# Bank order of the panels, and small work moved in its queues, in a two-layer decoder trunk

## The chip, the cores and the metric

One core of one Trainium2 chip. The metric is the device time of one execution in microseconds (us). Three runs of the kernel before gave 1307.50, 1307.45 and 1304.81: median 1307.45.

## What is computed

A decoder trunk of two layers on 512 tokens of width 1024, in float32. Layer one is gated linear attention, layer two stick-breaking attention on keys and values of its own projection; each is followed by a mixture of 16 experts (top group, two experts of it). Cut to what matters here:

```
def gla_mixer(u, w_in, w_gk2, b_gk2, o_norm, w_out):      # u = rms_norm(h, a_norm)
    q, k, v, gk_lr, g = split(u @ w_in, [512, 1024, 2048, 2064])
    gk = log_sigmoid(gk_lr @ w_gk2 + b_gk2) / 16           # gk_lr has 16 columns
    b = cumsum(gk) in chunks of 64
    q_dec, k_inv, k_to_end = q * exp(b) * 128**-0.5, k * exp(-b), k * exp(b_last - b)
    att = tril(q_dec @ k_inv.T)
    o = att @ v + q_dec @ state;  state = exp(b_last) * state + k_to_end.T @ v
    return (rms_norm(o, o_norm) * silu(g)) @ w_out
h = h + gla_mixer(...);  h = h + hier_moe(rms_norm(h, m_norm[0]), ...)
k1, v1 = split(rms_norm(h, kv_norm) @ w_kv)
h = h + stick_breaking(rms_norm(h, b_norm) @ b_w_q, k1, v1) @ b_w_out
h = h + hier_moe(rms_norm(h, m_norm[1]), ...);  out = rms_norm(h, final_norm)
```

## The kernel before

The program is written out by hand, one instruction stream for each engine, with semaphores between them. Every product of a large matrix is made of three: an operand is rounded to the type float32r (`hi`, by ACT) and its residual is kept as a second operand (`lo`, by DVE), and PE adds hi*hi, lo*hi and hi*lo (`three`, L1272). Weights come in blocks of 1 MB (4 tiles of 128 rows by 512 columns), loaded by SP into four slots `raw` (L411), rounded by ACT's `split` (L463) and completed by DVE's `split` (L811); the factor of the norm gain is multiplied in there, four instructions of 512 columns each. A weight without a gain takes one instruction of 2048 columns.

A panel is a product with 512 output columns: two blocks, 96 matmuls, and four PSUM banks. `dense(p, c, feature_major)` (L1340) computes panel p from blocks c and c+1 and writes banks 0 to 3 for even p and 4 to 7 for odd p. ACT's `panel_out_tokens` (L538) or DVE's `panel_out_features` (L879) copies it out, times the reciprocal norm: of a token for the first, by a row that is broadcast over the partitions (`rstd_row`) for the second. In layer one the panels are 0 (values, first half), 1 (queries), 2 (keys), 3 (values, second half), 4 and 5 (output gate), and 6 and 7 (output projection). The 16-column low-rank input of the forget gates is computed inside panel 0's function, and the gates (`wgk2`, L1382) after it, into banks 4 to 7, from where DVE adds the bias (L918).

The first panel of a layer is `dense_first` (L1317): token tiles of x (or h) are transposed by PE one at a time (`transposed_tile`, L1300), rounded by ACT (`tile_hi`, L529) and completed by DVE (`tile_lo`, L874), and each is followed by its two half products (blocks c and c+1, 12 matmuls each). Before the last tile's halves stands `between()`: in layer one the low-rank products and then the factor sums `rstd_row_sums` (L1309), in layer two the sums alone. The sums need the squares of all tokens (ACT, L522), the reciprocal root (ACT and DVE) and four diagonal tiles (DVE, L854); they write bank 6, and ACT copies the row out (L536). The products of panel 0 don't need them.

At the start ACT's queue issues nine small loads (L480): five rows of norm gains, then the low-rank weight `lr_raw`, `wgk2`, the gate bias `bgk` and `onorm`. PE first transposes the gains (L1362), then token tile 0. After layer one's panels come 16 transposes of the keys (L1398, banks 0 to 3) and 16 score products (L1405, banks 4 to 7); ACT copies the transposed keys (L595), DVE the scores (L950), which it writes over the untransposed keys. In layer two panels 12 and 13 are the two halves of the queries; DVE copies the second (L1202) behind the residual of block 13, and the early scores (`early_scores`, L1617) need only the first half, the late ones (`late_scores`, L1630) both.

Each engine takes its instructions in the order written; a wait holds all that stands behind it in the same queue.

## Time and profile before

| | |
|---|---|
| median of three runs | 1307.45 us |
| the profiled execution | 1304.74 us, span 1303.1 us |
| PE busy | 1136.8 us, 87% of the span |
| DVE, ACT, POOL busy | 819.4, 694.4, 157.1 us |
| granted PE clock, mean | 0.936 |
| moved by DMA | 283.49 MB, mean 218 GB/s |

The profile is of one execution. Its times count from the start of the span; 1.6 us lie around the span. An engine's idle time is put down to the instruction that released it. L12 is line 12 of the kernel before. In a row of the timeline the first number is the start and the second the time to the end of the group, x8 the number of records in it (a float32 matmul leaves more than one), and the bracket the idle time of the engine ahead of it with what ended it. The granted clock is the share of full speed that PE's throttle let through: 1.00 is 2.4 GHz, 0.50 is 1.2 GHz.

### The profile page before, as it was taken

What the parts mean: (1) busy time and instruction counts of PE and PEld (TensorE: products, weight loads), DVE (VectorE), ACT (ScalarE), POOL (GpSimd) and SP (SyncE); (2) the same over time, 40 slices, a digit from 0 to 9 for tenths busy, and PEclk for the clock granted to TensorE, in tenths of its full rate; (3) what the DMA queues carried; (4) which work ended last, traced back from release to release, by engine and by line L of the source; (5) the groups of instructions that cost most, each with busy time, mean ns of one, the idle gap of its engine ahead of it and who ended that gap; (6) DMA issues with size and microseconds to landing.
All of it is one profiled execution on the core that took longest, in us unless ns stands there. A gap on an engine that the chain in (4) does not pass through costs nothing.

```text
span 1303.1 us, 14486 instructions
## 1 busy us (share of the span) xinstructions
PE 1136.8 (87%) x5477; PEld 859.9 (66%) x5477; DVE 819.4 (63%) x825; ACT 694.4 (53%) x732; POOL 157.1 (12%) x169
## 2 busy tenths in 40 slices
PE   5799997974999999995799989999839999999970
PEld 4488875853677777774578867767626777777740
DVE  2454236266888888885523346662568888888846
ACT  2442433243777777775233226662427777777742
POOL 1100030012010100001100004430030010010004
PEclk9899998985999999998799988999859999999995
DMA  8343103207999999996412210003069999999925
GB/s 282 79 145 130 33 1 117 77 17 235 385 391 393 403 392 392 403 371 243 147 65 98 97 33 1 1 17 129 1 222 374 394 399 390 393 394 411 380 75 193
DMA packets 89060, 283.49 MB, mean 218 GB/s; under 512 B 11704, under 2 KB 11872, under 8 KB 89008
## 3 DMA queue, kind: packets, MB, share of 16 engines
q1 hardware_dynamic: 70272, 239.09, 48.5%
q0 software_dynamic: 11024, 39.07, 9.0%
q10 hardware_dynamic: 7712, 4.63, 1.1%
q8 instruction: 34, 0.56, 0.2%
q14 instruction: 18, 0.15, 0.0%
HBM read 259.96 MB, written 22.81 MB: 217 GB/s over the span
## 4 chain that ended last, share of the span: by engine, by line
PE 77%; DVE 7%; issue 5%; POOL 4%; ACT 3%; DMA 2%; ACTq 1%; POOLq 0%; DVEq 0%
PE ps L1274 23%; PE ps L1276 23%; PE ps L1275 23%; PE ps L1458 2%; PE ps L1292 1%; POOL xn_r L1829 1%; DMA xn<-output_table,pos 1%; PE ps L1419 1%; DVE h L1170 1%; PE ps L1486 1%; DVE raw L1214 1%; DVE xn_r L1218 1%; DMA pad<-normed_rows,token 1%; POOL xn_r L1824 1%; POOL pad_r L1824 1%
## 5 line engine op out<-in xcount | busy, mean ns | idle before, releaser
L816 DVE TENSOR_TENSOR w_lo<-raw,w_hi 128x2048 fp32r<-128x2048 f32 x72 | 164.7, 2289 | 94.8 <-ACT w_hi L470 94.6
L470 ACT CAST w_hi<-raw 128x2048 fp32r<-128x2048 f32 x72 | 137.7, 1912 | 117.7 <-PE ps L1276 117.5
L1274 PE MATMUL ps<-xT_hi,s_hi 128*96 128x512 f32 (+1 forms) x392 | 157.0, 400 | 8.6 <-DVE s_lo L910 5.2
L816 DVE TENSOR_TENSOR xT_lo<-raw,xT_hi 128x2048 fp32r<-128x2048 f32 x64 | 146.1, 2288 | 20.4 <-ACT xT_hi L470 20.4
L1274 PE MATMUL ps<-w_hi,s_hi 128*96 128x512 f32 x384 | 154.7, 403 | 4.6 <-DVE s_lo L992 4.6
L1276 PE MATMUL ps<-xT_hi,s_lo 128*96 128x512 f32 (+1 forms) x392 | 155.5, 397 | 0.0
L1275 PE MATMUL ps<-xT_lo,s_hi 128*96 128x512 f32 (+1 forms) x392 | 154.7, 395 | 0.0
L1276 PE MATMUL ps<-w_hi,s_lo 128*96 128x512 f32 x384 | 152.9, 398 | 0.0
L1275 PE MATMUL ps<-w_lo,s_hi 128*96 128x512 f32 x384 | 152.1, 396 | 0.0
L470 ACT CAST xT_hi<-raw 128x2048 fp32r<-128x2048 f32 x64 | 122.0, 1912 | 38.3 <-PE ps L1276 38.3
L1274 PE MATMUL ps<-w_hi,xT_hi 128*128 128x512 f32 x304 | 122.1, 401 | 12.9 <-DVE w_lo L820 6.4
L820 DVE SCALAR_TENSOR_TENSOR w_lo<-raw,gainT,w_hi 128x512 fp32r<-128x512 f32 x88 | 60.0, 746 | 114.8 <-ACT w_hi L474 114.8
L1275 PE MATMUL ps<-w_lo,xT_hi 128*128 128x512 f32 x304 | 120.3, 396 | 0.0
L1276 PE MATMUL ps<-w_hi,xT_lo 128*128 128x512 f32 x304 | 120.1, 395 | 0.0
L474 ACT ACTIVATE w_hi<-raw,gainT 128x512 fp32r<-128x512 f32 x88 | 56.1, 713 | 117.5 <-PE ps L1276 117.5
L816 DVE TENSOR_TENSOR w_lo<-xn,w_hi 128x2048 fp32r<-128x2048 f32 x32 | 73.4, 2292 | 28.9 <-ACT w_hi L470 28.9
L1274 PEld LDWEIGHTS ps<-xT_hi,s_hi 128*96 128x96 f32 (+1 forms) x392 | 63.4, 162 | 35.3 <-issue 6.7
L1274 PEld LDWEIGHTS ps<-w_hi,s_hi 128*96 128x96 f32 x384 | 63.4, 165 | 30.4 <-DVE s_lo L992 5.6
L816 DVE TENSOR_TENSOR xT_lo<-xn,xT_hi 128x2048 fp32r<-128x2048 f32 x32 | 73.4, 2292 | 15.7 <-ACT xT_hi L470 15.7
L1276 PEld LDWEIGHTS ps<-xT_hi,s_lo 128*96 128x96 f32 (+1 forms) x392 | 62.8, 160 | 28.6 <-issue 1.1
L1276 PEld LDWEIGHTS ps<-w_hi,s_lo 128*96 128x96 f32 x384 | 62.6, 163 | 27.5
L1275 PEld LDWEIGHTS ps<-xT_lo,s_hi 128*96 128x96 f32 (+1 forms) x392 | 63.1, 161 | 26.5 <-issue 0.9
(282 smaller groups left out, 2004.9 us busy)
## 6 DMA issues: line engine op xcount, KB each, us to landing
raw<-in_m_w_up SPq DMA_DIRECT2D x64, 1024.0 KB, 10.5
xn<-in_m_w_gate SPq DMA_DIRECT2D x60, 1024.0 KB, 11.6
raw<-in_m_w_down SPq DMA_DIRECT2D x60, 1024.0 KB, 11.2
raw<-in_a_w_in SPq DMA_DIRECT2D x12, 1024.0 KB, 5.9
output_table<-pad POOLq DMA_DIRECT2D x32, 384.0 KB, 6.4
raw<-in_w_kv SPq DMA_DIRECT2D x8, 1024.0 KB, 7.4
raw<-in_a_w_out SPq DMA_DIRECT2D x4, 1024.0 KB, 5.7
raw<-in_m_w_gate SPq DMA_DIRECT2D x4, 1024.0 KB, 8.8
```

The lines of the kernel that those rows point to most:

```text
L470: se.copy(hi, raw_block).then_inc(A["hi_done"], 1)
L474: ins = se.activation(hi[:, cols], raw_block[:, cols], ACT.Copy, scale=gainT[:, n:n + 1])
L816: ve.tensor_tensor(lo, raw_block, hi, ALU.subtract).then_inc(V["lo_done"], 1)
L820: ins = ve.scalar_tensor_tensor(lo[:, cols], raw_block[:, cols], gainT[:, n:n + 1], hi[:, cols], ALU.mult, ALU.subtract)
L1170: ve.scalar_tensor_tensor(h[:, i, :], y_rows[n], w12[:, k, i:i + 1], h[:, i, :], ALU.mult, ALU.add).then_inc(V["combined"], 1)
L1214: ve.scalar_tensor_tensor(zt[part], z_of(q, part), 0.0, zt[part], ALU.max, ALU.add).then_inc(V["L_done"], 1)
L1218: ve.tensor_tensor(L_of(L_lo, q, part), zt[part], L_of(L_hi, q, part), ALU.subtract).then_inc(V["L_lo_done"], 1)
L1274: te.matmul(o, a_hi, b_hi, start=start, stop=False)
L1275: te.matmul(o, a_hi, b_lo, start=False, stop=False)
L1276: return te.matmul(o, a_lo, b_hi, start=False, stop=stop)
L1458: ins = te.transpose(ps[:, 4 + f, CAP * k:CAP * (k + 1)], xg[:, slot, pair_columns(4 * f + k)], ident[0:CAP, 0:CAP])
L1824: ge.tensor_copy(L_of(L_hi, q, part), zt[part]).then_inc(G["L_hi_done"], 1)
```

## The change

Loads and transposes at the start: the four loads of the low-rank weight, `wgk2`, bias and `onorm` are issued by SP behind the x tiles and ahead of block 2, not by ACT. PE transposes token tile 0 before the gains, and ACT and DVE handle that tile before they need the gains. The rounding and residual of the low-rank weight come directly after block 1 on ACT and DVE, ahead of token tile 1. ACT's squares of a tile follow the rounding of the next one. In `dense_first` the low-rank products stay ahead of the last tile's halves and the factor sums go between the two halves, in both layers.

Bank order: layer one's panels are numbered 0, 2, 3, 4, 5, 6, so that queries go to banks 0 to 3, directly after the gates in banks 4 to 7, and all later ones alternate; each wait goes with its panel. The scores are computed before the keys are transposed, and DVE waits for the transposes before it writes scores over the keys. In layer two the second query copy stands ahead of the residual of block 13.

```diff
@@ sync
             for i in range(NT):
...

+            for dst, src in ((lr_raw, a_w_in[0, :, GK0:GK0 + RANK]...), (wgk2, a_w_gk2[0]),
+                             (bgk, a_b_gk2[0]...), (onorm, a_o_norm[0].partition_broadcast(P))):
+                sp.dma_start(dst, src).then_inc(A["small_loaded"], 16)
@@ scalar
-            load_small(loads, A["small_loaded"])
...
+            tile_hi(0, 0)
             act.wait_ge(V["gains_out"], 1)
-            tile_hi(0, 0)
             split(0)
             split(1)
+            act.wait_ge(V["lr_scaled"], 1)
+            se.copy(lr_hi, lr_raw[:, :, :]).then_inc(A["lr_hi_done"], 1)
             for i in range(1, NT):
                 tile_hi(0, i)
-            norm_squares(0)
-            act.wait_ge(V["lr_scaled"], 1)
-            se.copy(lr_hi, lr_raw[:, :, :]).then_inc(A["lr_hi_done"], 1)
+                squares_of(0, i - 1)
+            squares_of(0, NT - 1)
+            rsqrt_first(0, NT)
             split(2)
...
-            panel_out_tokens(3, 7, v[:, :, BN:2 * BN])
+            panel_out_tokens(4, 7, v[:, :, BN:2 * BN])
-            panel_out_tokens(4, 9, sg[:, :, 0:BN], ACT.Silu)
+            panel_out_tokens(5, 9, sg[:, :, 0:BN], ACT.Silu)
-            panel_out_tokens(5, 11, sg[:, :, BN:2 * BN], ACT.Silu)
+            panel_out_tokens(6, 11, sg[:, :, BN:2 * BN], ACT.Silu)
@@ vector
+            tile_lo(0, 0)
             dve.wait_ge(M["gains_tr"], 1)
             ve.tensor_copy(gainT[:, :], ps[:, 7, 0:5 * KT]).then_inc(V["gains_out"], 1)
             dve.wait_ge(V["gains_out"], 1)
-            tile_lo(0, 0)
             split(0)
             split(1)
-            for i in range(1, NT):
-                tile_lo(0, i)
             dve.wait_ge(A["small_loaded"], 16 * SMALL)
             ve.tensor_tensor(lr_raw...).then_inc(V["lr_scaled"], 1)
+            dve.wait_ge(A["lr_hi_done"], 1)
+            ve.tensor_tensor(lr_lo, lr_raw[:, :, :], lr_hi, ALU.subtract).then_inc(V["lr_lo_done"], 1)
+            for i in range(1, NT):
+                tile_lo(0, i)
             norm_scale(0)
             diagonals()
-            dve.wait_ge(A["lr_hi_done"], 1)
-            ve.tensor_tensor(lr_lo, lr_raw[:, :, :], lr_hi, ALU.subtract).then_inc(V["lr_lo_done"], 1)
             split(2)
...
-            panel_out_features(1, 3, qT, DK ** -0.5)
+            panel_out_features(2, 3, qT, DK ** -0.5)
-            panel_out_features(2, 5, kT)
+            panel_out_features(3, 5, kT)
...
             for n in range(8, 14):
                 split(n)
+            dve.wait_ge(M["ktok_tr"], 1)
             for i in range(NT):
                 dve.wait_ge(M["att_done"], i + 1)
...
             split(B + 12)
+            panel_out_features(13, B + 11, qT1[:, 4:8, :], SD ** -0.5)
             split(B + 13)
-            panel_out_features(13, B + 11, qT1[:, 4:8, :], SD ** -0.5)
@@ tensor
-            def dense_first(p, c, turn, event, between):
+            def dense_first(p, c, turn, event, first, between, between_half):
                 transposed_tile(turn, event, 0)
+                first()
                 for j in range(NT):
                     if j == NT - 1:
                         pe.wait_ge(V["xT_lo_done"], XT[turn] + NT)
                         between()
                     half(j, 0)
                     if j < NT - 1:
                         transposed_tile(turn, event, j + 1)
+                    else:
+                        between_half()
                     half(j, 1)
...
-            dense_first(0, 0, 0, 0, low_rank)
+            dense_first(0, 0, 0, 0, gains_transposed, low_rank, token_factors)
             pe.wait_ge(V["lr_out"], 1)
...
+            pe.wait_ge(A["panel_out"], 1)
+            dense(2, 2, True)
             pe.wait_ge(V["gates_in"], GH)
-            dense(1, 2, True)
-            pe.wait_ge(A["panel_out"], 1)
-            dense(2, 4, True)
+            dense(3, 4, True)
             pe.wait_ge(V["qk_out"], 1)
-            dense(3, 6, False)
+            dense(4, 6, False)
             pe.wait_ge(V["qk_out"], 2)
-            dense(4, 8, False)
+            dense(5, 8, False)
             pe.wait_ge(A["panel_out"], 2)
-            dense(5, 10, False)
-            pe.wait_ge(V["k_toend"], 1)
+            dense(6, 10, False)
+            pe.wait_ge(V["k_inv"], 1)
             pe.wait_ge(A["panel_out"], 3)
...
-                    ins = te.transpose(ps[:, i, P * j:P * (j + 1)], kT[:, j, P * i:P * (i + 1)], ident[:, :])
-            ins.then_inc(M["ktok_tr"], 1)
-            pe.wait_ge(V["k_inv"], 1)
-            pe.wait_ge(A["panel_out"], 4)
...
-            pe.wait_ge(V["k_inv"], 1)
-            pe.wait_ge(A["panel_out"], 4)
                     ins = te.matmul(ps[:, 4 + i, P * j:P * (j + 1)], kinv[:, j, t], qT[:, j, t], start=True, stop=True)
                 ins.then_inc(M["att_done"], 1)
+            pe.wait_ge(V["k_toend"], 1)
+            pe.wait_ge(A["panel_out"], 4)
...
+                    ins = te.transpose(ps[:, i, P * j:P * (j + 1)], kT[:, j, P * i:P * (i + 1)], ident[:, :])
+            ins.then_inc(M["ktok_tr"], 1)
...
-            dense_first(8, B, 3, 2, lambda: rstd_row_sums(2))
+            dense_first(8, B, 3, 2, lambda: None, lambda: None, lambda: rstd_row_sums(2))
```

## Rows read from the trace of the kernel before

**Rows 1.** The page, part 4: share of the chain that ended last, by engine.
```profile
PE 77%; DVE 7%; issue 5%; POOL 4%; ACT 3%; DMA 2%; ACTq 1%; POOLq 0%; DVEq 0%
```

**Rows 2.** Waits of PE over the whole span: total us, times, longest us.
```profile
PE ps L1362 <- DMA pad<-in_m_norm: 7.9, 1, 7.9
...
PE ps L1274 <- DVE s_lo L910: 5.2, 1, 5.2
PE ps L1608 <- DVE pad L883: 5.2, 1, 5.2
...
PE ps L1274 <- DVE pad L918: 2.8, 1, 2.8
...
PE ps L1313 <- DVE pad L854: 1.9, 1, 1.9
```

**Rows 3.** The chain in order of time, 0 to 90 us: start us, us, what.
```profile
3.16 0.43 ACTq L480
...
4.97 3.97 ACTq L480
8.97 1.20 ACT L557
10.27 1.01 ACT xT_hi L531
11.28 2.46 ACT w_hi L474 x4
13.76 2.75 DVE w_lo L820 x4
...
35.80 4.17 ACT xn L522 x8
41.46 0.88 DVE pad L854 x4
...
43.70 0.43 PE ps L1276
```

**Rows 4.** Time by engine, 87 to 174.5 us: busy us (count), clock, DMA share, GB/s.
```profile
87.00:174.50 87.50, 87.50 (x388) 72.42 (x387) 35.14 (x36) 27.78 (x40) 0.00 (x0) 1.00 0.19 61
```

**Rows 5.** Timeline of PE, 42 to 64 us: start, us, operation, idle before.
```profile
42.68 0.59 PE L1274 MATMUL ps<-xT_hi,s_hi 128*16 128x512 f32 x1 [5.17 <-DVE s_lo L910]
...
50.31 1.05 PE L1313 MATMUL ps<-pad,neg_one 128*128 128x128 f32 x8
...
56.75 3.70 PE L1382 MATMUL ps<-pad 16*128 16x512 f32 x8
63.27 0.80 PE L1274 MATMUL ps<-xT_hi,pad_r 128*128 128x512 f32 x1 [2.82 <-DVE pad L918]
```

**Rows 6.** Timeline of DVE, first and second layer's panels.
```profile
87.45 2.29 DVE L883 SCALAR_TENSOR_TENSOR pad<-ps,pad 128x2048 f32<-128x2048 f32 x1 [8.46 <-PE ps L1276]
...
770.68 2.29 DVE L816 TENSOR_TENSOR w_lo<-raw,w_hi 128x2048 fp32r<-128x2048 f32 x1 [8.57 <-ACT w_hi L470]
772.89 2.28 DVE L883 SCALAR_TENSOR_TENSOR pad<-ps,pad 128x2048 f32<-128x2048 f32 x1
```

**Rows 7.** Line L418, the four token tiles of x (issued 0.95 to 3.66).
```profile
DMA to landing us min/median/max: 3.7/11.0/12.2
```

**Rows 8.** Timeline of PE, 173 to 182 us.
```profile
174.29 1.91 PE L1398 MATMUL ps<-ident,pad 128*128 128x128 f32 x16
177.06 3.81 PE L1405 MATMUL ps<-pad 128*128 128x128 f32 x32 [0.86 <-ACT raw L542]
```

**Rows 9.** Line L414, weight blocks 0 and 1 (issued 1.39 and 1.86).
```profile
DMA to landing us min/median/max: 6.0/7.7/9.4
```

**Rows 10.** DMA issues, 0 to 80 us: name, queue, count, KB, us to landing.
```profile
pad<-in_a_o_norm ACTq DMA_DIRECT2D x1, 128.0 KB, 16.2
...
lr_raw<-in_a_w_in ACTq DMA_DIRECT2D x1, 64.0 KB, 13.3
```

**Rows 11.** Timeline of ACT: the copy of the first panel.
```profile
56.86 2.42 ACT L542 ACTIVATE pad<-ps,rstd 128x512 f32<-128x512 f32 x4
```

More of the change, by code:

```diff
@@ L421, in _ @@
                     load(streams[0][1], 1)
+            with nc.allow_non_contiguous_dma(reason="512 gate biases and 16 columns a row"):
+                for dst, src in ((lr_raw[:, :, :], a_w_in[0, :, GK0:GK0 + RANK].rearrange("(k p) r -> p k r", p=P)),
+                                 (wgk2, a_w_gk2[0]), (bgk[:, :], a_b_gk2[0].rearrange("(h p) -> p h", p=P)),
+                                 (onorm, a_o_norm[0].partition_broadcast(P))):
+                    sp.dma_start(dst, src).then_inc(A["small_loaded"], 16)
             for layer in range(LAYERS):
@@ L484, in _ @@
             load_small(loads, A["gains_loaded"])
-            loads = [(lr_raw[:, :, :], a_w_in[0, :, GK0:GK0 + RANK].rearrange("(k p) r -> p k r", p=P))]
-            loads += [(wgk2, a_w_gk2[0]),
-                      (bgk[:, :], a_b_gk2[0].rearrange("(h p) -> p h", p=P)),
-                      (onorm, a_o_norm[0].partition_broadcast(P))]
             router_loads = []
@@ L1357, in dense, with gains_transposed @@
                     ins.then_inc(M["blk_used"], 1)
+            def gains_transposed():
+                pe.wait_ge(A["gains_loaded"], 16 * 5)
+                te.transpose(ps[:, 7, 0:5 * KT], gain_rows, ident[0:5 * KT, 0:5 * KT]).then_inc(M["gains_tr"], 1)
             pe.wait_ge(G["consts"], 1)
-            pe.wait_ge(A["gains_loaded"], 16 * 5)
-            te.transpose(ps[:, 7, 0:5 * KT], gain_rows, ident[0:5 * KT, 0:5 * KT]).then_inc(M["gains_tr"], 1)
             def gate_input(k):
@@ L1375, in low_rank, with token_factors @@
                     gate_input(k)
+            def token_factors():
                 pe.wait_ge(G["consts"], 2)
                 rstd_row_sums(0)
-            dense_first(0, 0, 0, 0, low_rank)
+            dense_first(0, 0, 0, 0, gains_transposed, low_rank, token_factors)
             pe.wait_ge(V["lr_out"], 1)
@@ L1383, in _ @@
             ins.then_inc(M["gates_done"], 1)
+            pe.wait_ge(A["panel_out"], 1)
+            dense(2, 2, True)
             pe.wait_ge(V["gates_in"], GH)
-            dense(1, 2, True)
-            pe.wait_ge(A["panel_out"], 1)
-            dense(2, 4, True)
+            dense(3, 4, True)
             pe.wait_ge(V["qk_out"], 1)
-            dense(3, 6, False)
+            dense(4, 6, False)
             pe.wait_ge(V["qk_out"], 2)
-            dense(4, 8, False)
+            dense(5, 8, False)
             pe.wait_ge(A["panel_out"], 2)
-            dense(5, 10, False)
-            pe.wait_ge(V["k_toend"], 1)
+            dense(6, 10, False)
+            pe.wait_ge(V["k_inv"], 1)
             pe.wait_ge(A["panel_out"], 3)
-            for i in range(NT):
-                for j in range(GH):
-                    ins = te.transpose(ps[:, i, P * j:P * (j + 1)], kT[:, j, P * i:P * (i + 1)], ident[:, :])
-            ins.then_inc(M["ktok_tr"], 1)
-            pe.wait_ge(V["k_inv"], 1)
-            pe.wait_ge(A["panel_out"], 4)
             for i in range(NT):
@@ L1406, in _ @@
                 ins.then_inc(M["att_done"], 1)
+            pe.wait_ge(V["k_toend"], 1)
+            pe.wait_ge(A["panel_out"], 4)
+            for i in range(NT):
+                for j in range(GH):
+                    ins = te.transpose(ps[:, i, P * j:P * (j + 1)], kT[:, j, P * i:P * (i + 1)], ident[:, :])
+            ins.then_inc(M["ktok_tr"], 1)
             ktok = gate
```

## The prediction

> **What bounds the kernel now.** The first view is the page's chain of work that ended last: 77% of it is PE, and no other engine has more than 7% [rows 1]. So time is won where PE stands still, or where it runs at the lower of its two clock levels; work taken off ACT or DVE counts only if PE waits for it. The second view, PE's waits, shows where it stands still near the edited lines [rows 2]: 7.9 us at the very start until the norm gains have landed; 5.2 us before the low-rank product, which waits for the small weight's residual (L910); 2.8 us before panel 1, which waits for the gates to be read out of banks 4 to 7 (L918); in the second layer 1.9 us before the factor sums (L1313), and 5.2 us before the late scores (L1608), which wait for the second query copy. Each is a single wait, so each can be priced by itself.
>
> The third view is the chain in order of time for the first 90 us [rows 3]. It shows what stands ahead of the first matmul: ACT's queue issues the small loads from 3.16 us and is held by the last until 8.94, then loads its function table (1.2), rounds token tile 0 (1.0), rounds block 0 (2.5), and DVE forms the residual (2.75): PE's first product starts at 16.5. Later it shows four squares of 4.2 us together, and factor tiles that end at 42.3, just ahead of the low-rank product.
>
> **The clock.** From 87 to 174.5 us PE is busy without a gap at a granted clock of 1.00, and four panels of 96 products take 87.5 us [rows 4], 0.228 each: that is the 2.4 GHz level. Behind the 5.2 us of idle time a product took 0.43 [rows 3], the 1.2 GHz level, and the 24 low-rank products lasted from 42.68 to 50.31, 7.6 us [rows 5]. At 0.228 they take 5.5, so the drop cost 2.2. Behind the 2.8 us of idle time panel 1 lasted from 63.27 to its copy at 87.45 [rows 5, 6], 24.2 us where 96 times 0.228 is 21.9: 2.3 lost.
>
> **The change, part by part.**
>
> *Start.* Four loads leave ACT's queue, and PE transposes token tile 0 before the gains. The table load can begin near 3.2 and ends by 4.5. Token tile 0 lands at 0.95 + 3.7 = 4.65 [rows 7]. Eight transposes at the lower level: 16 took 1.91 at the full one [rows 8], so 8 take 1.9 here, to 6.6. ACT rounds the tile until 7.6; DVE's residual of the tile, half of a 2.29 us operation [rows 6] and a little, ends near 8.9. The gains still land at 7.9 [rows 2] on the same queue, are transposed by 8.2 and copied by DVE after the tile, to 9.1. Block 0 landed at 7.4 and block 1 at 11.3 [rows 9], and block 1 is wanted at 11.6. So 9.1 + 2.5 + 2.75 [rows 3] puts the first product at 14.5 in place of 16.5: 2.0 won. The bounds: 0 if the gains land over 2 us later, 3 if DVE's two steps are hidden. I take 2.0, by the durations.
>
> *Small loads in SP's queue.* They now stand behind x tiles 1 to 3 and ahead of blocks 2 and 3. The last x tile lands at 3.66 + 12.2 = 15.9 [rows 7]. Blocks 2 and 3 are wanted only after 36 us, so their delay costs nothing. The small loads cost nothing if they are in before ACT is wanted for token tile 1: in the new order DVE has finished block 1 at 14.5 + 2.75 = 17.2, scaling and splitting the low-rank weight takes about 0.9 on both engines, and PE's first half block (12 products, 2.7 to 5.1 us at the two levels) and the transposes end between 18 and 20.5. The limit for landing is therefore about 19. I take the loads of one queue to land in the order of their issue, as the x tiles do (3.7 us for the first, 12.2 at the most). With 0.2 MB behind the 15.9 I expect 17 to 18.5, cost 0; it was 13.3 to 16.2 us from issue to landing for two of them on ACT's queue, beside the large loads [rows 10], and that is the upper bound: 29 to 32 us. Behind a late landing, token tile 1's rounding on ACT and its residual on DVE would both queue, and PE behind them. The Trainium skill (DMA: Bandwidth & Descriptors, Queues, rings and completion order) speaks against this move: each queue has its own ring on an engine, rings are served in turn and each one in its own order, so a small load in a queue of its own shares from the first packet, and one behind 4 MB waits for them. By it the loads land behind the last x tile and not before, where in their own queue they could have come sooner; the sum by it is the same as long as they make the limit. The trace agrees on the turns only in part: the separate queue still needed 13 to 16 us.
>
> *Low-rank split and squares moved ahead.* The weight's residual is ready before 20 us, and token tile 3's residual before PE gets there, so the 5.2 us wait goes, and with it the 2.2 of lower clock. Next late would be the factor sums. On the old time axis PE is through with its third tile at 37.5, low-rank ends at 43.0, the first half of tile 3 (12 products) at 45.7. Of the 4.2 us of squares, half now lies beside PE's work, so the factor tiles end near 40.2 rather than 42.3 [rows 3]: covered by 5 us. The sums (0.9) end at 46.6; ACT's copy of the row factor and DVE's scaling of the low-rank result (together about 1.3, an estimate from their 512 columns) end at 47.9, and PE needs them at 49.3.
>
> *Panel 2 before 3.* The gate products take 3.7 [rows 5], to 53.0. The query panel goes into banks 0 to 3, which ACT must have emptied: row factor copied at 47.2, block 3 rounded (2.5) by 49.7, panel copy (2.42 [rows 11]) by 52.2. That is 0.8 ahead of PE. The wait of 2.8 goes, and 2.3 of lower clock. If the cover fails, PE waits by the excess alone. DVE, though, starts the gate chain only 7.5 us earlier (53.0 for 60.5) while the panel's end comes 12.5 earlier; it had 8.46 idle before its copy [rows 6], so 3.4 are left and nothing is late. The later panels keep the alternation they had, and their copies shift with them.
>
> *Scores before key transposes.* The transposes took 1.91 and the scores 3.81 [rows 8]. Scores now start at once, and transposes end 174.4 + 3.8 + 1.9 = 180.1. ACT comes to the transposed keys after a panel copy (2.4), a block (1.9) and a table (1.2), at about 180.0. DVE's new wait for the transposes stands before its attention copies, behind a block that it finishes later than 180.1. I charge 0.2; bounds 0 and 0.5. The 0.86 and the following 1 us of PE's idle time become one gap of 2.
>
> *Second layer.* The factor sums move behind a half tile (2.7 us), which covers the 1.9 wait [rows 2]: 1.9 won. The second query copy (2.28) goes ahead of a block residual that waited for ACT: before, 770.68 + 2.29, then the copy to 775.17 [rows 6]; ACT's rounding began 1.9 before 770.68, at 768.8, so now 768.8 + 2.28 + 2.29 = 773.4. The attention chain starts 1.8 earlier. PE's late scores start 4.2 earlier, but DVE leads that chain: I take 1.8, bounds 0 and 3 (a better clock in the first pair).
>
> **The sum.** 2.0 + 5.2 + 2.2 + 2.8 + 2.3 - 0.2 + 1.9 + 1.8 = 18.0. The profiled execution took 1304.7 (span 1303.1 and 1.6 around it), which gives 1286.7; the median of the three runs is 1307.45, 2.7 higher, which gives 1289.4. I state 1288. A measurement of this kernel can tell about 0.2%, 2.6 us.
>
> **The rivals.**
> 1. *Small loads late* (13%, of which 3% slower than before). Place: DVE's wait before the low-rank scaling. Price: 1 us for each us past 19. At the bound of 29 to 32 it is 10 to 13: 1298 to 1301. It ends slower only from a landing past 37, and by over 0.2% past 40: 1310. For it: 13 to 16 us on the old queue. Against it: only 0.2 MB, and no large load beside it in another queue.
> 2. *The clock falls in the attention of layer one* (12%), at the merged gap of 2 us. For it: the drop behind 2.8. Against it: in the second layer 1.9 of waiting cost no visible drop. Price one or two drops of 2.2: 1290 to 1292.5.
> 3. *The clock terms do not come*, because a cover of 0.8 or 3.4 us fails and new short waits stand there (10%): 4.5 less, 1292.5.
> 4. *It does not do what it says*: the gain is given back, since a later stage is tied to loads (3%): 1305 to 1308. Against it: the loads wait for slots that DVE frees, and the chain has 2% DMA [rows 1].
> 5. *More than forecast* (5%): 1282 to 1284, by the upper bounds of start and query copy.
>
> The forecast itself has 57%: 1285 to 1291. With rivals 2, 3 and 5 and the nearer half of rival 1 the range is 1282 to 1296. Faster 0.94, same 0.02, slower 0.04 (3% of rival 1, 1% unforeseen).
>
> **What would show it.** First product near 14.5; no wait at L910 or L918; low-rank products all near 0.23; first query copy on DVE near 73 in place of 87.45; DVE's first absolute value after the second query copy 1.8 earlier relative to the panel's end. Wrong: a wait of PE or ACT behind the low-rank scaling, a product of 0.43 behind a panel boundary, or a first layer that is less than 12 us shorter.

## The result, and the profile after

| | before | changed |
|---|---|---|
| median of 4 runs each | 1306.27 us | 1290.05 us (1289.15 to 1291.36) |
| the profiled execution | 1304.74 | 1291.36 |
| its span, granted clock | 1303.1, 0.936 | 1289.7, 0.939 |

The ratio is 0.9877, interval 0.986 to 0.9894: the change makes the kernel faster by 16.2 us by the medians. The profiled execution of the changed kernel is the slowest of its four and that of the kernel before lies below its median, so the two traces differ by 13.4 us only; the landmarks below are accounted against that. A landmark is the start of one step that both kernels have. The page of the changed kernel, part 1 (busy time of each engine) and part 4 (the chain):

```profile
PE 1134.4 (88%) x5477; PEld 859.7 (67%) x5477; DVE 819.5 (64%) x825; ACT 694.4 (54%) x732; POOL 156.2 (12%) x169
...
PE 79%; DVE 7%; issue 5%; POOL 4%; DMA 3%; ACT 3%; POOLq 0%; DVEq 0%; ACTq 0%
```

PE's share of the chain is 79% where it was 77 [rows 1], ACT's queue is at 0%. PE's waits of the changed kernel, the answers to [rows 2]:

```profile
PE ps L1661 <- POOL xn_r L1839: 6.8, 1, 6.8
PE ps L1277 <- DVE w_lo L822: 6.6, 1, 6.6
...
PE ps L1309 <- DMA h<-in_x: 4.4, 1, 4.4
...
PE ps L1429 <- ACT pad L597: 2.2, 1, 2.2
...
PE ps L1618 <- DVE pad L885: 1.0, 1, 1.0
```

None is left on the low-rank residual, on the gates or on the factor tiles. The late scores of the second layer wait 1.0 in place of 5.2. In exchange the first factor product of the second layer's first pair waits 6.8 for POOL (1.9 before), and the state products of layer one wait 2.2 in one piece for ACT's copy of the transposed keys.

The timeline of PE, changed kernel, the start (start us, us, line, shape, count, idle before), answering to [rows 5]:

```profile
14.27 0.80 PE L1277 MATMUL ps<-w_hi,xT_hi 128*128 128x512 f32 x1 [6.55 <-DVE w_lo L822]
...
19.55 1.41 PE L1309 MATMUL ps<-ident,h 128*128 128x128 f32 x8
...
36.26 0.40 PE L1277 MATMUL ps<-xT_hi,s_hi 128*16 128x512 f32 x1
...
44.57 1.05 PE L1316 MATMUL ps<-pad,neg_one 128*128 128x128 f32 x8
...
48.28 4.52 PE L1392 MATMUL ps<-pad 16*128 16x512 f32 x8
52.74 0.79 PE L1277 MATMUL ps<-xT_hi,pad_r 128*128 128x512 f32 x1
...
57.95 0.40 PE L1277 MATMUL ps<-xT_hi,pad_r 128*128 128x512 f32 x1
```

The first product starts at 14.27 (16.56 before). The first half block and the transposes last until 20.71. The low-rank products follow at 36.26 without a wait and take 5.57 to 41.83, at 0.23 each. The gate products start at 48.28 (56.75), the query panel at 52.74 (63.27), directly behind them. But its first products again take 0.43, and only from 57.95 do they take 0.23. The same stretch by windows (PE busy, PEld, DVE, ACT, POOL, granted clock, DMA share, GB/s):

```profile
48.28:52.74 4.46, 4.46 (x10) 1.49 (x9) 2.74 (x4) 2.72 (x5) 0.69 (x1) 0.81 0.05 6
52.74:57.95 5.21, 5.21 (x14) 4.11 (x13) 5.02 (x5) 0.02 (x1) 3.74 (x6) 0.51 0.96 317
57.95:76.30 18.35, 18.35 (x82) 15.20 (x81) 9.50 (x9) 9.99 (x8) 2.05 (x4) 1.00 0.80 239
```

Already in the gate products the clock falls, at 100% PE busy: 0.81, then 0.51, then 1.00. For the kernel before, the same places are in the prediction's rows: gate products of 3.70, a wait of 2.82, and then a slow start of the panel.

The shift of each landmark, changed against before, in the two profiled executions:

| landmark | before | changed | shift |
|---|---|---|---|
| first product | 16.56 | 14.27 | 2.3 |
| low-rank products start | 42.68 | 36.26 | 6.4 |
| gate products start | 56.75 | 48.28 | 8.5 |
| query panel starts | 63.27 | 52.74 | 10.5 |
| DVE copies the queries | 87.45 | 77.20 | 10.25 |
| DVE copies the scores | 180.94 | 170.69 | 10.25 |
| first addition to the residual stream | 248.41 | 238.37 | 10.0 |
| layer two, first token transposes | 625.00 | 615.69 | 9.3 |
| layer two, first absolute value | 775.09 | 761.43 | 13.7 |
| the same step of the second pair | 794.34 | 781.39 | 12.95 |
| last scaling of the output | 1291.82 | 1278.45 | 13.4 |

The small loads: SP's queue and DVE's timeline of the changed kernel.

```profile
4.48 6.77 SPq L426 DMA_DIRECT2D pad<-in_a_w_gk  x1
...
12.37 0.51 SPq L426 DMA_DIRECT2D pad<-in_a_o_norm  x1
```

```profile
11.47 5.39 DVE L822 SCALAR_TENSOR_TENSOR w_lo<-raw,gainT,w_hi 128x512 fp32r<-128x512 f32 x8 [2.70 <-ACT w_hi L479]
16.78 0.28 DVE L905 TENSOR_TENSOR lr_raw<-lr_raw,gainT 128x128 f32<-128x128 f32 x1
```

The broadcast of the output norm, the last of them, is issued at 12.37 and lands 4.4 later, at 16.8. DVE starts to scale the low-rank weight at 16.78, with no idle time behind block 1: the loads were in just in time. The issue of `wgk2` held SP for 6.77 us, which delayed nothing that was wanted.

In the second layer DVE now does the query copy (L885) first and the residual second, answering to [rows 6]:

```profile
756.91 2.29 DVE L885 SCALAR_TENSOR_TENSOR pad<-ps,pad 128x2048 f32<-128x2048 f32 x1 [6.59 <-PE ps L1279]
759.12 2.28 DVE L818 TENSOR_TENSOR w_lo<-raw,w_hi 128x2048 fp32r<-128x2048 f32 x1
761.43 1.22 DVE L1211 TENSOR_SCALAR raw<-ps 128x1024 int32<-128x1024 int32 x1
```

The first absolute value (L1211) comes 4.5 us after the first of the two, as before (770.68 to 775.09). But the copy can start when PE has ended the panel, where the residual had to wait for ACT's rounding.

### The profile page after: what moved, and what is told of

Read it like the earlier page. It is cut to its first block, busy times and chain, and to the rows that moved or that the text cites. A ratio compares the mean times of both kernels' runs of the same rounds, so it can differ in the third digit from the quotient of the medians.

```text
span 1289.7 us, 14486 instructions
## 1 busy us (share of the span) xinstructions
PE 1134.4 (88%) x5477; PEld 859.7 (67%) x5477; DVE 819.5 (64%) x825; ACT 694.4 (54%) x732; POOL 156.2 (12%) x169
## 4 chain that ended last, share of the span: by engine, by line
PE 79%; DVE 7%; issue 5%; POOL 4%; DMA 3%; ACT 3%; POOLq 0%; DVEq 0%; ACTq 0%
PE ps L1277 24%; PE ps L1279 23%; PE ps L1278 23%; PE ps L1468 2%; PE ps L1295 1%; POOL xn_r L1839 1%; DMA xn<-output_table,pos 1%; PE ps L1429 1%; DVE h L1173 1%; PE ps L1496 1%; DVE raw L1217 1%; DMA pad<-normed_rows,token 1%; DVE xn_r L1221 1%; POOL xn_r L1834 1%; POOL pad_r L1834 1%
## 5 line engine op out<-in xcount | busy, mean ns | idle before, releaser
L818 DVE TENSOR_TENSOR xT_lo<-raw,xT_hi 128x2048 fp32r<-128x2048 f32 x64 | 146.1, 2288 | 20.7 <-ACT xT_hi L475 20.6
L1279 PEld LDWEIGHTS ps<-w_hi,s_lo 128*96 128x96 f32 x384 | 62.6, 163 | 27.3
```

What stands on the lines that cost most here:

```text
L818: ve.tensor_tensor(lo, raw_block, hi, ALU.subtract).then_inc(V["lo_done"], 1)
L1279: return te.matmul(o, a_lo, b_hi, start=False, stop=stop)
```

## The experiments

Every experiment is an edit of the changed kernel, and its time is a median of four or five runs unless another number stands there. Each profiled execution is read by the same landmarks, since the medians of several differ by less than they vary; a landmark is then one trace's, and where several kernels share a stretch that no edit touches, their spread is given. The gap from the start of the gate products to DVE's copy of the queries is called the query stretch below. At full clock it would be 3.6 for the gate products + 21.9 for 96 products = 25.5; before it was 30.7, and 28.9 in the changed kernel.

**The bank order undone.** Panels 1 to 5 again, key transposes ahead of the scores, no wait of DVE on them.

```diff
-            pe.wait_ge(A["panel_out"], 1)
-            dense(2, 2, True)
             pe.wait_ge(V["gates_in"], GH)
-            dense(3, 4, True)
+            dense(1, 2, True)
+            pe.wait_ge(A["panel_out"], 1)
+            dense(2, 4, True)
```

> The changed kernel with the bank order of before (queries in banks 4 to 7 behind the gates, key transposes ahead of the scores). Theory A (the gate products themselves, 16 of 128 rows, lower the clock; the wait behind them does not): panel of the queries starts about 2 us later, as the 2.8 us wait comes back and the gate products take 3.7 instead of 4.45, and its first 10 to 12 products run at 0.43 as they do without the wait; 2 to 2.5 us slower than the changed kernel, 1292 by the median. Theory B (the prediction's: the wait lowers the clock, and in the changed kernel something else happened to lower it): the panel's loss is not the same in both, and the cost is 3 us or more beyond the wait, or none at all.

Measured: 1293.62 us, ratio to before 0.9905 (0.9888 to 0.9921), 3.6 more than the changed kernel. By windows, the gate products and the first products of the panel:

```profile
48.10:51.80 3.70, 3.69 (x9) 1.40 (x8) 2.74 (x4) 2.72 (x5) 0.06 (x1) 1.00 0.00 0
54.61:60.32 5.71, 5.71 (x13) 4.51 (x14) 2.27 (x1) 3.37 (x2) 4.13 (x7) 0.50 1.02 333
```

The wait of 2.82 is back, between the two windows. The query stretch is 31.3, 2.4 longer than in the changed kernel: of the 2.8 + 2.3 that I had given to the new bank order, only about 2.4 is there. (In four other traces with the new bank order and 16-row gate products the stretch is 27.3 and not 28.9; by those it is 4.0.) The gate products run at full clock here and the products behind the wait do not. The clock is lost once, with or without the wait.

**The low-rank split back in its old place** on ACT and DVE, behind all token tiles. DVE's part of the edit:

```diff
+            for i in range(1, NT):
+                tile_lo(0, i)
             ve.tensor_tensor(lr_raw...).then_inc(V["lr_scaled"], 1)
-            dve.wait_ge(A["lr_hi_done"], 1)
-            ve.tensor_tensor(lr_lo...)
-            for i in range(1, NT):
-                tile_lo(0, i)
             norm_scale(0)
             diagonals()
+            dve.wait_ge(A["lr_hi_done"], 1)
+            ve.tensor_tensor(lr_lo...)
```

> The changed kernel with the rounding and residual of the low-rank weight back behind the last token tile, the squares and the small loads left as changed. Expected: residual at about 39.5 us, so PE waits some 3.2 us before the low-rank products. Theory A (idle time behind full products lowers the clock as before): some 10 of the 24 low-rank products at 0.43, 2.2 more; 5.4 us slower, 1295.5. Theory B (the drop of the kernel before there needed its longer wait of 5.2): products at 0.23, 3.2 us slower, 1293.3.

Measured: 1296.22 us, 0.9923 (0.9906 to 0.9939). The timeline of PE, the low-rank products:

```profile
39.44 0.39 PE L1277 MATMUL ps<-xT_hi,s_hi 128*16 128x512 f32 x1 [3.13 <-DVE s_lo L912]
...
40.13 0.54 PE L1277 MATMUL ps<-xT_hi,s_hi 128*16 128x512 f32 x1
40.47 0.63 PE L1278 MATMUL ps<-xT_lo,s_hi 128*16 128x512 f32 x1
...
43.46 0.48 PE L1279 MATMUL ps<-xT_hi,s_lo 128*16 128x512 f32 x1
```

The wait is 3.13 rather than 5.2, since the squares stay spread between the tiles. Three products still run at 0.23, the fourth takes 0.34 and the next seven 0.43, though PE works again. The gate products start at 53.0 rather than 48.3: 3.1 of waiting and 1.6 of clock. So wait and clock term of this step are both real. Behind that, 1.6 came back in the query stretch (27.3) and 3.1 went in the state products of layer one (see below), which makes about the 6.1 by which its span is longer. The query stretch holds a second reading:

```profile
53.02 3.70 PE L1392 MATMUL ps<-pad 16*128 16x512 f32 x8
...
57.55 0.63 PE L1277 MATMUL ps<-xT_hi,pad_r 128*128 128x512 f32 x1
```

The gate products run at full clock (3.70) and no wait follows them. The first products of the panel, from 56.65, still take 0.23, and from 57.55 on seven take 0.43. So the fall can come behind the 16-row products as well as in them.

**The second query copy late again**, behind the residual of block 13.

```diff
-            panel_out_features(13, B + 11, qT1[:, 4:8, :], SD ** -0.5)
             split(B + 13)
+            panel_out_features(13, B + 11, qT1[:, 4:8, :], SD ** -0.5)
```

> The changed kernel with the second query copy behind the residual of block 13 again. Expected on DVE: the first absolute value of layer two 1.9 us later relative to the end of panel 13. Theory A (PE's long wait before the first sums, 6.8 us in the changed kernel, costs 0.7 in clock in the first pair): by the second pair the difference is 1.2. Theory B (DVE leads the whole chain): it stays 1.9.

Measured: one run of 1288.35. From the token transposes of layer two to the first absolute value it took 147.8, where it took 145.7 in the changed kernel (145.7 to 146.4 over all that have the early copy and no filler in layer two): the copy is worth about 1.8 there, 2.1 by these two traces. But from there to the second pair, which I call the first pair's time, it took 17.7 in place of 20.0, and the sum is 165.5 in place of 165.7. By these two traces, what DVE wins is lost again within 20 us. How much of it is lost in general is less sure: the kernel before, with the late copy too, took 19.25 for the first pair, and the nine traces with the early copy and no filler there took 18.8 once and 20.0 to 20.3 otherwise.

**The small loads back on ACT's queue.**

```diff
@@ sync (the four loads)
-                    sp.dma_start(dst, src).then_inc(A["small_loaded"], 16)
@@ scalar (behind the load of the gains)
+            load_small([(lr_raw...), (wgk2...), (bgk...), (onorm...)], A["small_loaded"])
```

> The changed kernel with the four small loads issued by ACT at its start, as before. Theory A (ACT's table load behind the held queue was what set the start): table load at 9 us again, token tile 0 rounded at 10.3, first product at 17.3 or later, 3 us later than in the changed kernel; the small loads landing at 16 to 21 us then hold the low-rank rounding on ACT and with it token tile 1, up to 1 us more. Theory B (the gains and block 0 set the start anyway): first product within 0.5 us of 14.3.

Measured: one run of 1294.39. ACT's timeline and DVE's:

```profile
4.98 3.88 ACTq L480 DMA_DIRECT2D pad<-in_a_o_norm  x1
8.89 1.28 ACT L555 ACT_TABLE_LOAD   x1 [8.73 <-issue]
10.19 1.01 ACT L529 CAST xT_hi<-ps 128x1024 fp32r<-128x1024 f32 x1
12.60 5.02 ACT L474 ACTIVATE w_hi<-raw,gainT 128x512 fp32r<-128x512 f32 x8 [1.40 <-DVE gainT L898]
```

```profile
15.27 5.39 DVE L820 SCALAR_TENSOR_TENSOR w_lo<-raw,gainT,w_hi 128x512 fp32r<-128x512 f32 x8 [2.71 <-ACT w_hi L474]
21.62 0.29 DVE L903 TENSOR_TENSOR lr_raw<-lr_raw,gainT 128x128 f32<-128x128 f32 x1 [0.96 <-DMA pad<-in_a_o_norm]
```

ACT's queue is held for 3.88 us again, so its table is loaded at 8.89 and tile 0 is rounded at 10.19; the first product starts at 18.06, 1.5 later than before the change, since the gains now come behind tile 0. And the loads themselves are late: DVE waits 0.96 for them until 21.6. The low-rank products start 3.9 later than in the changed kernel. The last of the small loads, the broadcast of `onorm`, arrives sooner behind 4 MB in one queue (16.8) than in a queue of its own (21.6); the low-rank weight itself arrives at 15.9 and 16.5. The queue is not the only difference: here SP issued blocks 2 and 3 at 4.11 and 4.63, so 6 MB ran beside the small loads, while in the changed kernel those blocks are issued from 12.93, behind them.

**Gate products with all 128 rows.** The rows above 16 of the weight are zero and those of the low-rank result one, set by POOL, for which SP waits before the small loads and DVE before it writes the low-rank result; the sums are the same.

```diff
-                ins = te.matmul(ps[:, 4 + i, :], wgk2[:, DK * i:DK * (i + 1)], lrT, start=True, stop=True)
+                ins = te.matmul(ps[:, 4 + i, :], wgk_all[:, DK * i:DK * (i + 1)], lr_all, start=True, stop=True)
+            link(ge.memset(wgk_all, 0.0), ge.memset(lr_all, 1.0))
```

> The changed kernel with gate products over all 128 rows: the weight's rows past 16 hold zeros and the moving operand's ones, so the same four products of 512 columns give the same gates in the same passes. Theory A (few rows in use lower the clock): no drop, gate products 3.7 us as before the change, the query panel's products at 0.23 from the first, 0.7 + 2.3 = 3 us faster than the changed kernel, 1287. Theory B (the drop is one of float32 operands, or of the exchange of the engines behind it, not of rows): products at 0.43 behind the gates as in the changed kernel, 1290.

Measured: 1288.2 us, 0.9866 (0.9834 to 0.9899). The windows of the gate products and of the panel's first products:

```profile
47.39:50.42 3.03, 3.03 (x9) 1.35 (x8) 2.49 (x4) 2.81 (x5) 0.00 (x0) 1.00 0.00 0
50.42:55.60 5.18, 5.18 (x24) 4.11 (x23) 4.79 (x6) 0.00 (x0) 3.27 (x5) 1.00 0.69 195
```

Same columns, same count, same place in the kernel, and the clock stays at 1.00. The query stretch is 25.4, which is the full-clock value. So the 16-row products cost the clock here, not idle time: PE had none. It isn't one lucky trace: all three kernels with 128 rows have 25.4, and all eight with the new bank order and the four 16-row products in one burst have 27.3 or 28.9 (four each). The median is 1.9 below the changed kernel's, but the intervals overlap; in this trace 1.4 was lost again in the state products of layer one.

**Gate products spread between the panel's products**, one behind each of its first groups of three.

```diff
-            for i in range(GH):
-                ins = te.matmul(... wgk2[:, DK * i:DK * (i + 1)], lrT, ...)
-            ins.then_inc(M["gates_done"], 1)
-            dense(2, 2, True)
+            dense(2, 2, True, gate_product)
```

> The changed kernel with each of the four gate products placed behind one of the first four groups of three products of the query panel (banks 4 to 7 against 0 to 3), all else the same. Theory A (a stretch of 4 us with few rows is what lowers the clock; spread out it does not): products at 0.23 throughout, gates done 2 us later, which DVE's idle time before the query copy covers; 3 us faster than the changed kernel, 1287. Theory B (any such product counts, or DVE's chain is then late): 0 to 1 us, or slower.

Measured: 1302.19 us (10 runs), 0.9969 (0.9953 to 0.9984), 12 slower than the changed kernel. Timeline and windows of PE:

```profile
51.08 0.76 PE L1277 MATMUL ps<-xT_hi,pad_r 128*128 128x512 f32 x1 [2.75 <-issue]
...
52.62 2.07 PE L1394 MATMUL ps<-pad 16*128 16x512 f32 x2
```

```profile
45.00:48.30 3.30, 3.30 (x18) 2.50 (x16) 0.68 (x1) 2.67 (x5) 0.00 (x0) 1.00 0.67 257
51.08:56.00 4.92, 4.92 (x8) 2.12 (x8) 0.37 (x1) 0.00 (x0) 3.06 (x5) 0.50 0.68 180
56.00:60.00 4.00, 4.00 (x7) 1.54 (x7) 0.00 (x0) 0.00 (x0) 2.78 (x5) 0.50 1.04 345
```

Two things went wrong. PE now stands for 2.75 us at the panel's start: the four gate products had covered ACT's copy of panel 0, which ends at 51.0 in both kernels. And the clock is at 0.50 from the first product behind that wait, all through the gate products and until about 71, so the panel takes 36.3 us where gate products and panel took 28.9 together. The kernel shows the cover that I had sized at 0.8 us, from its other side: in the changed kernel that copy ends at 51.0 and PE is there at 52.74, or would be at 51.9 had the gate products kept full clock.

It shows one thing more. Ahead of the wait stand only full products at 1.00, and no 16-row product has run yet; the first three products behind it run at the low level. So a wait of 2.75 lowered the clock by itself here.

**Filler ahead of the first product.** 26 transposes of the identity into a free bank, behind the gains.

```diff
+                for i in range(26):
+                    te.transpose(ps[:, 3, P * (i % 4):P * (i % 4 + 1)], ident[:, :], ident[:, :])
```

> The changed kernel with 26 transposes of the identity into bank 3 (not used until panel 0 clears it) in PE's 6.5 us of idle time before the first product. Theory A (the low clock of panel 0's first products comes from the idle time before them): first products at 0.23 and the first half block in 2.8 instead of 5.3 us, 2.5 to 2.8 us faster than the changed kernel, 1287.5, even if the first product starts up to 0.3 later. Theory B (the first rise needs full products, or the half block then waits for block 1's residual at 16.9 or token tile 1): under 1 us faster.

Measured: 1289.88 us, 0.9872 (0.9838 to 0.9905). The first product came at 14.66, like the 14.5 to 14.7 of the other experiments that leave the start alone (14.27 in the first trace), and the products behind it took 0.23 at once, though 1.75 us lie between filler and first product; the low-rank products start at 33.88, 2.4 earlier. The gain is there at that point but not in the median: in its trace the stretch with the state products of layer one was 1.4 longer.

**Filler ahead of the first pair of layer two.** 26 products into a free bank, behind the early scores.

```diff
+            for i in range(26):
+                te.matmul(ps[:, 7, :], neg_tri[:, :], xT_hi[:, i % KT, :], start=True, stop=True)
```

> The changed kernel with 26 products of 512 columns into bank 7 (free until the first values) in PE's 6.8 us of idle time before the sums of the first head pair in layer two. Theory A (those sums run at the low clock because of the wait, and late scores of the next pair behind them lead): sums and scores in 6 instead of 9.6 us; up to 3 us faster, but bounded by DVE's and POOL's chain, so 1.5 to 3. Theory B (chain of DVE and POOL leads): within 0.5.

Measured: 1286.42 us, 0.9847 (0.9816 to 0.9878), 3.6 less than the changed kernel, though the intervals overlap. Its timeline of PE, then the window of the pair's sums, then the same window of the changed kernel:

```profile
765.24 6.17 PE L1699 MATMUL ps<-xT_hi,neg_tri 128*128 128x512 f32 x26
772.30 0.45 PE L1661 MATMUL ps<-pad_r,neg_tri 128*128 128x384 f32 x1 [0.89 <-POOL xn_r L1841]
```

```profile
772.30:778.50 6.20, 5.42 (x37) 5.01 (x38) 4.53 (x5) 3.85 (x5) 1.54 (x2) 1.00 0.00 0
```

```profile
769.68:779.30 9.62, 9.62 (x42) 9.17 (x42) 5.32 (x5) 4.10 (x5) 4.03 (x4) 0.56 0.00 0
```

The first pair's sums run at 1.00 in place of 0.56, and the pair takes 17.5 in place of 20.0. This is where the gain of the second query copy goes: PE came to the sums sooner, had waited longer (6.8, against 2.25 with the late copy and 1.9 before), and ran them at 0.56 (0.77 and 0.62 there). With filler in the idle time the sum over this part of layer two is 163.4 in place of 165.7.

Its trace also shows the state products of layer one, here (second fence) against the changed kernel (first):

```profile
171.68 2.96 PE L1429 MATMUL ps<-pad 64*128 64x256 f32 x16 [2.16 <-ACT pad L597]
174.57 1.99 PE L1439 MATMUL ps<-pad 128*128 128x256 f32 x8
176.50 1.94 PE L1447 MATMUL ps<-pad 128*64 128x256 f32 x8
```

```profile
171.79 3.80 PE L1429 MATMUL ps<-pad 64*128 64x256 f32 x16 [2.16 <-ACT pad L597]
175.52 3.78 PE L1439 MATMUL ps<-pad 128*128 128x256 f32 x8
179.23 2.60 PE L1447 MATMUL ps<-pad 128*64 128x256 f32 x8
```

Behind the same gap of 2.16 us the one runs at 2.96, 1.99 and 1.94, the other at 3.80, 3.78 and 2.60. Nothing in the edit touches this place.

**The changed kernel again**, without an edit, to see how far one trace can be trusted.

> The changed kernel once more, unedited, as the measure for the three beside it. In the profiles so far that have its order of scores and key transposes, the stretch from the copy of the scores to the first addition of layer one's output took 67.7 us in three, 69.0 in two and 70.8 in three; with the order of before it took 67.5 and 67.7. Theory A (the merged 2.2 us of PE's idle time lowers the clock in some executions): one of these values, and runs that spread over 3 us, 1289 to 1292. Theory B (an effect of the edits in those kernels): 67.7.

Measured: 1291.32 us (5 runs, 1289.29 to 1294.61), 0.9891 (0.9874 to 0.9908). That is 14.7 less than the 1305.97 of the kernel before in the same set of runs, where the first comparison gave 16.2. Its landmarks repeat the first trace's: low-rank 21.98 after the first product (21.99), query stretch 28.95 (28.92), first pair 20.2 (19.96). The stretch from the copy of the scores to the first addition is 67.53 (67.68). Over all nine profiled executions with the new order of scores and transposes, this stretch was 67.5 to 67.7 in four, 69.0 in two and 70.8 in three; in the two with the old order 67.5 and 67.7.

**Key transposes between the third and fourth score**, which halves the gap; the residual of block 13 moves behind the key copy on ACT and into the state chain on DVE.

```diff
-            for i in range(NT):
+            for i in range(3): scores(i)
+            ... (key transposes)
+            scores(3)
```

> The changed kernel with the key transposes between the third and the fourth score tile, and ACT's copy of the transposed keys ahead of its table-free rounding of block 13 (DVE's residual of block 13 goes behind the state update of chunk 1). Theory A (the gap matters): PE's idle time before the state products falls from 2.2 to about 1, no 0.43-level products there, keys copied 1 us earlier: stretch 67.7 us or less in the profile, 1 us faster by the path and up to 3 by the clock: 1287 to 1289. Theory B (the gap has no part in it, or block 13 then comes late): within 1 us of the changed kernel, or slower.

Measured: 1289.35 us, 0.9886 (0.9868 to 0.9903). Timeline of PE:

```profile
168.38 2.96 PE L1435 MATMUL ps<-pad 64*128 64x256 f32 x16 [1.06 <-ACT pad L596]
...
183.66 1.94 PE L1453 MATMUL ps<-pad 128*64 128x256 f32 x8 [1.83 <-DVE pad L965]
```

The gap is 1.06 and the clock holds, but a new wait of 1.83 stands in the third group of state products: DVE does the residual of block 13 ahead of that update. The stretch from the copy of the scores to the first addition is 69.3, which is no better than the mean of the nine, 69.0; and the median is 2.0 below the repeat's in the same set of runs, with intervals that overlap. No gain is shown for it on its own.

**Full rows, this order, and both fillers together.**

```diff
+            link(ge.memset(wgk_all, 0.0), ge.memset(lr_all, 1.0))
+            scores(0..2), key transposes, scores(3)
+            26 transposes ahead of the first product, 26 products ahead of the first pair
```

> The changed kernel with the full rows in the gate products, the transposes between the scores, and idle PE time filled before the first product and before the first pair's sums. If the terms add up: 1 to 3 (rows), 2 to 2.5 (start), 1 to 3 (scores), 2 to 3 (first pair) faster than the changed kernel, 6 to 9 in all: 1281 to 1284. If the clock's gains exclude one another in the first stage (rows and start both end before the same panel): 1285.

Measured: 1283.23 us (1282.45 to 1284.4), 0.9832 (0.9819 to 0.9846), 6.8 less than the changed kernel and 8.1 less than its repeat in the same set of runs; it and the next are the best of all, and here the intervals do not overlap. Which part gives how much is read from the landmarks, not from the medians. Low-rank products start at 33.96, the queries are copied at 71.29 (77.20), the first pair takes 17.5, the span's clock is 0.947.

**The same with filler ahead of layer two's first products** (45 transposes, and 12 behind the first token tile).

```diff
-            dense_first(8, B, 3, 2, lambda: None, lambda: None, lambda: rstd_row_sums(2))
+            fill(45)
+            dense_first(8, B, 3, 2, lambda: fill(12), lambda: None, lambda: rstd_row_sums(2))
```

> As e11_full_rows_warm, and PE's idle time before layer two's first panel filled too: 45 transposes of the identity behind the expert stage and 12 behind the first token tile's. Theory A: the first half block of that panel at 0.23, 2 us faster than e11_full_rows_warm. Theory B (the filler is longer than the wait, or ends too early to hold the clock): the same within 1 us, or slower by the overrun.

Measured: 1283.43 us (1280.19 to 1285.2), 0.9828 (0.9812 to 0.9845): no difference in the medians. Timeline of PE:

```profile
600.80 7.92 PE L1373 MATMUL ps<-ident 128*128 128x128 f32 x45 [7.08 <-POOLq L1840]
...
611.95 1.47 PE L1373 MATMUL ps<-ident 128*128 128x128 f32 x12
...
617.05 0.63 PE L1284 MATMUL ps<-w_hi,xT_lo 128*128 128x512 f32 x1
```

PE still stands for 2.3 us before and 2.3 behind the second filler. The first four products run at full clock, the fifth takes 0.35, and the next seven 0.43; without filler all twelve were slow. From the first addition of layer one to the second token transposes of layer two it took 385.8, where the kernel without this filler took 387.1, so 1.2 was won here. Its trace lost 1.8 elsewhere: the first products of the output projection ran at 0.43, behind idle times of 6.35 and 2.02 that are as long (6.34 and 1.93) in the other kernel, where they ran at 0.23. Whether filler without the two gaps would have won more was not tried.

## Why the prediction was right and where it failed

The forecast was 1288.0 in a range of 1282 to 1296; 1290.05 was measured, 2 us above. The number came out nearer than the mechanism. The sum was 18.0 against the profiled execution, where 13.4 came; by the medians it was 16.2, and 14.7 in the repeat. Layer one was to be 14.3 shorter and is 10.0 shorter; the query copy was to start near 73 and starts at 77.20. Two of the signs that the prediction had named as wrong are there: products of 0.43 behind a panel boundary, and a first layer less than 12 us shorter. That the median lies near 1288 all the same is in part luck: the median gained more (16.2) than the profiled executions (13.4) and than the repeat (14.7), and 1288 was set between a sum from the profiled time (1286.7) and one from the median of three runs (1289.4). Term by term, from the landmarks of the two traces:

| step | predicted | in the traces |
|---|---|---|
| start, and low-rank wait | 2.0 + 5.2 | 2.3 + 5.2, less 1.1 |
| low-rank clock | 2.2 | 2.1 |
| gates wait | 2.8 | 2.8, less 0.8 |
| query panel's clock | 2.3 | -0.3 |
| scores before transposes | -0.2 | 0 to the scores, -0.2 behind |
| between the layers | 0 | -0.7 |
| factor sums, second query copy | 1.9 + 1.8 | 4.4 |
| first pair, rest | 0 | -0.7, +0.4 |

*Start.* Right: 14.27 for 14.5. In these two traces the clock rose at about 20 us in both kernels, so of work begun 2.3 sooner more ran at the low level: the first half block and the transposes took 6.4 where they had taken 5.2. That loss isn't fixed: with the same start, the time from the first product to the low-rank products (less a wait) is 20.7 to 20.9 in three of nine traces and 21.5 to 22.0 in six. The filler kernel shows the other side: with PE at work ahead of the first product, the low-rank products start 2.4 sooner.

*Low-rank wait and its clock.* Right, both; undoing the step brings back a wait and seven slow products.

*Query panel's clock.* This is the step that failed: "the wait of 2.8 goes, and 2.3 of lower clock". I had put the slow products behind panel 1's start down to the 2.8 us of idle time ahead of them, because they stood behind it. With the wait gone they were still there; with 128 rows in the gate products they were gone. The cause that remained in the changed kernel is the four 16-row products: eight traces with them lost 1.8 or 3.4 us, three with 128 rows nothing. The other half of the step, that a wait of 2.8 lowers the clock, holds: the spread gate products have a wait of 2.75 with no 16-row product ahead of it, and in that one trace the products behind it ran at the low level. So each cause lowered the clock without the other; in the kernel before both stood there and the loss was paid once, and the change took away one. (Full rows with the old bank order was not tried.) Rival 3 had said that the clock terms would not come, because a cover fails. One of them did not come, and no cover had failed. The gate products themselves lost 0.8 of the step too, since the fall now came inside them.

*Gates' cover of ACT's copy.* Right, that ACT's copy of panel 0 ends just ahead of PE; the spread gate products turned that cover into a wait of 2.75.

*Small loads.* Rival 1 fell: they were in at 16.8, earlier than the 17 to 18.5 I took from the issue order, and the experiment on ACT's queue shows 21.6.

The Trainium skill (DMA: Bandwidth & Descriptors, Queues, rings and completion order) has rings served in turn and each in its own order; by that the separate queue could have been sooner. In the two kernels here its last small load was later by 4.8 us and the low-rank weight by 0.6, so the measurement decides for this kernel. It is no test of the turns alone, since 2 MB more ran beside the small loads there.

*Scores before transposes.* 0.2 was right for the time to the scores, and in the first trace for the whole. Rival 2, the fall of the clock at the merged gap, is real and comes in some executions only: in five of nine profiled ones, at 1.4 or 3.2 us, where one or two drops were priced at 2.2 or 4.4. It was given 12%; it is a coin toss. So the new order, which I priced at 0.2, costs about 1.4 on average of these nine (two times 1.4 and three times 3.2, over nine), as far as two traces of the old order without a fall can serve as the measure.

*Second layer.* The factor sums were worth 2.2 for 1.9 and the query copy about 1.8 to 2.1 for 1.8 at the place I had named. What I had not followed is the next step: the sums of the first pair are led by POOL, PE's wait before them grew, and the clock took back some or all of what DVE had won. With the copy late this part of the layer took the same time in one trace (165.5 and 165.7); against the kernel before, only 0.7 was taken back. With filler ahead of the sums it takes 163.4.

*Between the layers* 0.7 went, in the expert stage. From the first addition to layer two's first transposes the other experiments, which edit nothing there, take 376.1 to 377.1; the two traces here took 376.6 and 377.3. So most of the 0.7 is how this stretch varies.

## What to carry to other kernels

Where products run slow behind a wait, look at the last work before it too: here a burst of products with 16 of 128 rows lowered the clock with PE fully busy, and padding the rows to 128 gave back the 1.8 to 3.4 us that the other kernels lost there. A time won on an engine ahead of a wait of PE may be paid back in clock, so read on to the next landmark where both kernels do the same before a gain is booked; idle time of PE that can't be closed can be filled with products into a free bank, to close before the work that follows: gaps of 0.9 and 1.75 us behind the filler kept full clock here, one of 2.3 us kept it for four products only. Before work is taken from between two panels, ask which copy of another engine it covers.

## What the runs showed of the hardware that was not expected

- PE, 100% busy in 16-row products, was granted 0.81 of the clock in them and 0.51 behind them; with 128 rows it was 1.00 in both windows. In three other traces it was 1.00 in the 16-row products and fell only behind them.
- Behind 3.1 us of idle time three products, and behind 2.3 us four, ran at 0.23 before seven ran at 0.43; behind 2.75 us the first was slow.
- The same gap of 2.16 us lowered the clock in five of nine executions, in two sizes (1.4 and 3.2 us).
- Four small loads issued behind 4 MB in the same queue had all landed at 16.8, and in another queue beside 6 MB at 21.6; their issue held SP for 6.77 us in the one case, ACT for 3.88 in the other.
